# A weight sum of the gate-and-up units: formed by an accumulating transfer instead of by a VectorE addition

## What is computed

```python
D_MODEL = 1024
D_FF = 2816
def swiglu(h, w_gu, w_d):
    gu = h @ w_gu                                   # 1024 x 5632
    return (jax.nn.silu(gu[..., :D_FF]) * gu[..., D_FF:]) @ w_d

    # once in each layer
    hp = hp + swiglu(rms_norm(hp, norm_ffn[layer]), w_gate_up[layer], w_down[layer])
    hs = hs + swiglu(rms_norm(hs, norm_ffn[layer]), w_gate_up[layer], w_down[layer])
```

## Time and profile before

| | us |
|---|---|
| median of 3 timed runs | 1315.87 |
| lowest and highest of them | 1315.61, 1326.59 |
| the profiled execution, its time | 1321.13 |
| the profiled execution, its span from the first to the last instruction | 1319.6 |

### The profile page before, as it was taken

The page is one execution under the profiler, slowest core; times in us unless marked ns, Lnnn a source line. Parts: engine busy times, 40 slices in busy tenths (PEclk is TensorE's granted clock), DMA queues, the critical chain, the costliest instruction groups (busy, mean ns, idle before and its releaser), DMA issues.

```text
span 1319.6 us, 26871 instructions
## 1 busy us (share of the span) xinstructions
PE 1223.9 (93%) x10559; PEld 1008.9 (76%) x10559; DVE 1054.8 (80%) x1741; ACT 685.8 (52%) x1179; POOL 357.2 (27%) x571
## 2 busy tenths in 40 slices
PE   8999996999999889999999999999689999998997
PEld 7767585787787767778888888887568787787886
DVE  6446667899999967777877878777579999998885
ACT  6243556455555544336554655545555555654543
POOL 1004312100001124446455554553211000011230
PEclk9999997999999999999999999999989999998998
DMA  8658545777777699421133231232357777766992
GB/s 265 213 186 278 154 144 104 200 186 166 197 175 160 131 208 225 95 87 58 34 97 97 65 97 45 85 97 81 112 145 192 204 178 168 194 148 124 203 184 78
DMA packets 126230, 193.37 MB, mean 147 GB/s; under 512 B 7801, under 2 KB 88953, under 8 KB 121882
## 3 DMA queue, kind: packets, MB, share of 16 engines
q1 hardware_dynamic: 96730, 157.06, 37.8%
q0 software_dynamic: 29376, 34.61, 18.2%
HBM read 180.53 MB, written 11.11 MB: 145 GB/s over the span
## 4 chain that ended last, share of the span: by engine, by line
PE 52%; DVE 23%; ACT 11%; issue 6%; DMA 6%; POOL 1%; DVEq 0%; SPq 0%; ACTq 0%; POOLq 0%
PE P L2487 20%; PE P L2536 10%; PE P L2114 7%; DVE wl L1706 7%; ACT wh L1027 4%; DMA arena<-w_gu 3%; DMA arena<-w_dn 3%; DVE arena L1751 2%; PE P L2725 2%; ACT arena L1061 2%; DVE wl L1442 1%; DVE arena L1770 1%; DVE wl L1892 1%; PE P L2711 1%; PE P L2545 1%
## 5 line engine op out<-in xcount | busy, mean ns | idle before, releaser
L2487 PE MATMUL P<-arena,wh 128*128 128x260 f16 x2288 | 399.5, 280 | 51.3 <-DVE arena L1725 23.7
L2487 PE MATMUL P<-arena,wl 128*128 128x260 f16 x1144 | 319.2, 279 | 0.0
L2487 PEld LDWEIGHTS P<-arena,wh 128*128 128x128 f16 x2288 | 223.5, 99 | 100.8 <-issue 32.7
L1027 ACT ACTIVATE wh<-arena 128x1024 f16<-128x1024 f32 (+2 forms) x138 | 123.2, 897 | 136.3 <-PE P L2487 103.4
L2487 PE MATMUL P<-zh,wh 128*128 128x260 f16 x704 | 193.6, 275 | 0.0
L2487 PE MATMUL P<-zh,wl 128*128 128x260 f16 x704 | 192.5, 273 | 0.0
L2487 PE MATMUL P<-zl,wh 128*128 128x260 f16 x704 | 192.4, 273 | 0.0
L1706 DVE SCALAR_TENSOR_TENSOR wl<-arena,wh 128x1024 f16<-128x1024 f32 (+2 forms) x138 | 144.7, 1048 | 33.2 <-ACT wh L1027 32.7
L1706 DVE SCALAR_TENSOR_TENSOR wl<-stage,wh 128x1024 f16<-128x1024 f32 (+2 forms) x116 | 132.0, 1139 | 8.1 <-ACT wh L1027 7.6
L1027 ACT ACTIVATE wh<-stage 128x1024 f16<-128x1024 f32 (+2 forms) x116 | 114.0, 984 | 32.4 <-PE P L2487 25.1
L2487 PEld LDWEIGHTS P<-arena,wl 128*128 128x128 f16 x1144 | 113.0, 99 | 18.9
(11 more groups left out here) (422 smaller groups left out, 2656.3 us busy)
## 6 DMA issues: line engine op xcount, KB each, us to landing
arena<-w_gu SPq DMA_DIRECT2D x56, 512.0 KB, 6.2
stage<-w_in SPq DMA_DIRECT2D x23, 1024.0 KB, 5.3
stage<-w_gu SPq DMA_DIRECT2D x44, 512.0 KB, 5.0
arena<-w_gu POOLq DMA_DIRECT2D x22, 512.0 KB, 5.6
stage<-w_gu POOLq DMA_DIRECT2D x22, 512.0 KB, 7.5
arena<-w_dn SPq DMA_DIRECT2D x28, 384.0 KB, 5.5
arena<-w_dn SPq DMA_DIRECT2D x30, 320.0 KB, 4.9
arena<-cache_k SPq DMA_DIRECT2D x32, 256.0 KB, 3.6
```

The costliest lines, as they stand in the source:

```text
L1027: nc.scalar.activation(ringh[:, o:o + block_words(n)], source(kind, n), ACT.Copy, scale=WS).then_inc(c_hi, 1)
L2487: mm = nc.tensor.matmul(bank, w[:, o:o + 128], x[:, k, :], start=(i in (0, 1, 3) and k == a and w is ringh and x is xh), stop=(k == z - 1 ...
```

## The change

For the gate-and-up units (n < 11) T4 is no longer added by VectorE. GpSimd issues a transfer that adds B21 from memory onto T2 in place, the same kind as for T1 and T3. It waits for the low part of T2(n) (`c_lo`), and, since it counts on the same semaphore as T1's transfers, for all transfers of T1 and T4 that stand before it, T1(n+1) last. It stands at the head of iteration n of GpSimd's loop, ahead of T3(n+1) and T1(n+2); T1(n+2) now waits for T4(n) to have landed. ScalarE's high part of T4 waits for the transfer instead of for VectorE. The down units keep the VectorE addition. The load of B21 by SyncE stays, as B21 is an operand by itself too. The counts on `t_sum` and `t1_sum` are renumbered accordingly.

```diff
+SUMS = [(k, n) for n in range(NU) for k in ("T2", "T4") if k == "T2" or n >= NG]
+SUM_AT = {x: i + 1 for i, x in enumerate(SUMS)}
+ADDS = [("T1", 0), ("T1", 1)] + [(k, m) for n in range(NU) for k, m in (("T4", n), ("T1", n + 2))
+                                 if m < NU and (k == "T1" or n < NG)]
+ADD_AT = {x: i + 1 for i, x in enumerate(ADDS)}
...
-                if kind == "T1":
-                    pool.wait_ge(ld1[n % 2], first_load(n % 2, n, layer))
-                    if layer + n > 0:
-                        pool.wait_ge(t1_sum, 16 * (NU * layer + n))
+                if kind in ("T1", "T4"):
+                    if kind == "T1":
+                        pool.wait_ge(ld1[n % 2], first_load(n % 2, n, layer))
+                    else:
+                        pool.wait_ge(c_lo, NB7 * layer + 7 * n + 3)
+                    earlier = len(ADDS) * layer + ADD_AT[kind, n] - 1
+                    if earlier > 0:
+                        pool.wait_ge(t1_sum, 16 * earlier)
                     arrived = t1_sum
...
-                nc.gpsimd.dma_start(rows_of(kind, n), block_of({"T1": "B11", "T3": "B22"}[kind], n, layer),
+                nc.gpsimd.dma_start(rows_of(kind, n), block_of({"T1": "B11", "T3": "B22", "T4": "B21"}[kind], n, layer),
                                     accum_op=ADD).then_inc(arrived, 16)
...
                 for n in range(NU):
+                    if n < NG:
+                        second_term("T4", n, layer)
                     second_term("T3", n + 1, layer)
                     second_term("T1", n + 2, layer)
...
+                elif kind == "T4" and n < NG:
+                    act.wait_ge(t1_sum, 16 * (len(ADDS) * layer + ADD_AT["T4", n]))
                 else:
-                    act.wait_ge(t_sum, 2 * NU * layer + 2 * n + (1 if kind == "T2" else 2))
+                    act.wait_ge(t_sum, len(SUMS) * layer + SUM_AT[kind, n])
...
                 low_part(m, layer)
-                if i == 2:
+                if i == 2 and n >= NG:
                     weight_sum("T4", n, layer)
```

More of the change, by code:

```diff
@@ L1016, in convert @@
                 elif kind == "T1":
-                    act.wait_ge(t1_sum, 16 * (NU * layer + n + 1))
+                    act.wait_ge(t1_sum, 16 * (len(ADDS) * layer + ADD_AT["T1", n]))
                 elif kind == "T3":
@@ L1679, in weight_sum @@
                 if kind == "T2":
-                    dve.wait_ge(t1_sum, 16 * (NU * layer + n + 1))
+                    dve.wait_ge(t1_sum, 16 * (len(ADDS) * layer + ADD_AT["T1", n]))
                     dve.wait_ge(ld2[n % 2], first_load(n % 2, n, layer))
```

## The result

The kernel after takes 1330.88 us (median of 13 runs, 1325.78 to 1336.05), the kernel before, run as often beside it, 1320.97 us (1315.61 to 1329.24). The ratio is 1.008, 95% interval 1.006 to 1.0099: the change costs some 10 us. A later series of runs gave 1.0075 (1.0044 to 1.0106).

A forecast was written before the change was run, and what follows sets the result against it. VectorE was taken to bound the gate-and-up units, TensorE 1.2 us behind. Twenty steady periods at -0.6 us in all and +4 us for the units 0 gave +3.4 us on 1315.87: 1319 us, range 1300 to 1341.

The forecast's parts named there:

- VectorE sets the period, and the addition costs 1.32 us of it: Gate-and-up units: VectorE bounds the 20.33 us period; without the T4 addition VectorE alone would allow 19.01 us.
- the floor of 19.12 us: Gate-and-up units: TensorE, 1.21 us behind VectorE, lets the period fall from 20.33 to 19.12 us and no further.
- T4's transfer waits for T1(n+1), and VectorE for the transfer: Steady units: T1(n+1) must land before T4's transfer goes; VectorE then stands still 1.3 us, giving its saving back.
- R: Time to landing of T4's transfer in a gate-and-up unit: between 5.5 and 7.7 us, taken as 5.5.
- S: Start of TensorE's product i = 6 in a unit; T4's transfer must land by S + 6.99 or VectorE stands still.
- T1's delay of 1.0 us: Steady units: T4's transfer pushes T3's into T1's loads, delaying T1 by 1.0 us, between 0 and 2.5.
- The relation: Steady units, P being the period: 2P = 34.13 + R plus T1's delay, giving 20.3 us, ends 19.8 and 22.2.
- T3's delay costs nothing: Steady units: T3's transfer runs some 2 us later behind T4's, landing near S + 12.7, due only some 13.6 us after.
- The unit 0: First unit of each layer: late T4(0) costs +3.3 us in layer 1, +1.4 in layer 0; +4 taken.
- Ten periods of one kind: Ten periods in each layer, all counted as steady: 20 x (20.3 - 20.33) = -0.6 us.
- crowding: Rival: transfers crowd each other, landing takes 7.0 us and T1 is delayed 1.5; period 21.3, 1341 us; chance 0.25.
- The full gain: Rival: T4's transfer lands before S + 6.99, period 19.12 us, result 1294 us; chance 0.15, full or most of it.

The follow-up runs named there:

- e1: kernel after with neither transfer nor addition of T4 in the gate-and-up units (output lacks that part): 1294.84 us, ratio 0.9825 to the kernel before.
- e4: as e3, with VectorE's product of gate and up moved ahead of T4's low part: 1310.83 us, ratio 0.9915 to the kernel before.
- e7: e4 with the VectorE addition of T4 kept in unit 0 of each layer: 1305.14 us, ratio 0.9893 to the kernel before.
- e10: e4 with the VectorE addition of T4 kept in units 0 and 1 of each layer: 1298.34 us, ratio 0.9824 to the kernel before.
- e3: kernel after with a semaphore of its own for T4's transfer, so it doesn't wait for T1(n+1): 1316.78 us, ratio 0.9967 to the kernel before.
- e11: the kernel before, unchanged, run once more for a second profile: 1314.76 us.
- e8: the kernel after, unchanged, run once more for a second profile: 1331.05 us, ratio 1.0075 to the kernel before.
- e9: kernel after with the VectorE addition of T4 kept in units 0 and 1 of each layer: 1320.64 us, ratio 0.9996 to the kernel before.
- e2: as e1, but B21's bytes are fetched and added onto unused memory, and nothing waits: 1304.14 us, ratio 0.9878 to the kernel before.

## Why the prediction was right, and where it was not

The forecast was +3.4 us, no change within 1%, range 1300 to 1341. Measured: +10 us, 1330.88 us. Sign and class are right, the size is short by 7 us. The kernel before itself came out at 1320.97 in 13 runs, where the forecast started from 1315.87 in 3, so the difference is the fairer measure than the 12 us between 1319 and 1330.88.

- *VectorE sets the period, and the addition costs 1.32 us of it.* Right: 19.01 us was worked out, and 19.0 is the period of e1. The step to it from the 2.47 us of two low parts doesn't hold, as those two start 1.25 us apart; the 1.14 us that was used is the distance from the addition to the next instruction. And the floor of 19.12 us that TensorE was said to set is none: e1 has 18.99, and e4, e7 and e10 have units of 18.87.
- *T4's transfer waits for T1(n+1), and VectorE for the transfer.* Right. The chain of after runs through a load and two transfers, and taking the wait away (e3) shortens the steady periods from about 20.35 to 20.1 and 19.6 us.
- *R.* 5.5 us was taken; 5.94 is measured at 324.03, and the issue is 2.3 us after S. A landing at S + 8.2 against S + 6.99 due gives 1.2 us; VectorE waits 1.33 and 1.72, forecast 1.3.
- *T1's delay of 1.0 us.* Its loads go at 309.16 and it lands at 315.56 + 7.94 = 323.50: 14.3 us against 14.0 before. So the delay is 0.3. The relation also has 0.05 us between T1's landing and T4's issue, where the trace has 0.53 in 16 of 20. With all three in it, 2P = 34.13 + 0.5 + 5.9 + 0.3, P is 20.4; measured 20.35 on average, forecast 20.3. That the forecast came within 0.05 us is partly luck: the three errors of the sizes nearly cancel, and single periods differ by up to 1.9 us.
- *T3's delay costs nothing.* T3 goes right behind T4, 7.4 to 7.8 us to landing instead of 5.5, and ScalarE is shown waiting for it nowhere in the steady units of either profile.
- *The unit 0.* +4 us was forecast for the two heads, from +3.3 and +1.4. Against the very profile that it was worked out from, the heads are +3.6 and +0.3, and the step for layer 1 was good: 6 us of waiting forecast, 6.38 seen. But that profile had a long head in each layer; against the means of both profiles of before they are +6.2, and against the usual 15.4 us layer 1 alone has 6.1 and 6.4. In the first profile ScalarE waited 3.28 us for T3(1) in layer 1, in e11 0.33. The term was short because one profile's head was taken for the head.
- *Ten periods of one kind.* This is the step that failed. The sum took the period from unit 0 to unit 1 as a steady one, worth -0.03 us; it is 21.2 to 22.6 instead of 19.2 to 19.6, +5.4 us for the two. The prediction followed the late T4(0) into VectorE's low parts, and no further than the head. It also holds up ScalarE's copies, and with them TensorE, which stood still for 5.28 us and then ran its next product in 4.97 us at a clock of 0.51 instead of some 2.6. In layer 1 of e8 the chain of waits runs through TensorE alone from the end of this stop to the end of the first period. In after it goes from the slow product to the low part of T2(1) and so to T4(1), which was late once more (VectorE idle for 3.24 us). What the clock's share is, some 2 us in a layer by the rows, is an estimate: no run leaves the stop and not the fall. The timed runs of e9 show that undoing units 0 and 1 takes the loss back, its profile that this came from the heads, and e7 beside e10 that unit 1 has its own share in layer 1.

Of the rivals, crowding is not what holds up the steady units of the change: T1 and T3 can land late for nothing (e2, 151.9 us with the bytes and without), and T4 itself lands in 5.5 to 6.0 us there but for one unit. It is at work at the head, where 5.3 us came with the bytes in e2. And it comes up in the steady units once T4 no longer waits for T1: in e3, e4 and e10 T4's 7 us and more to landing are what is left. The full gain was wrong for the change, and not as a limit: once the wait for T1 is gone, VectorE has other work and the head is left alone, e10 gets a ratio of 0.9824, and the forecast's 1294 us were 0.983 of 1315.87.

The Trainium skill, DMA: Bandwidth & Descriptors, section Anatomy of one DMA — SWDGE (gpsimd) path, would have 3.2 us by its formula for the 512 KB of such a transfer, which is an estimate. The trace doesn't agree: in the steady units of before and after the shortest time to landing of such a transfer is 5.4 us.

## What to carry to other kernels

Moving work from a full engine to a transfer gives little as long as the consumer stands at the same place of the full engine's queue (+10 us here, and with the wait for T1 gone 0.3% less than before). Put the queue's independent work into the time of landing, and look at what shares a semaphore with the new transfer: a count shared by two streams is a wait of one for the other. Once that wait is gone, the two streams can run at the same time and each take longer; look at the time to landing again. Price the first two units of a pipeline by themselves, through the queue of every engine that the late operand holds up, and from more than one profile: here undoing 4 of 22 places took the whole loss back in the timed runs. And count what a stop of TensorE leaves behind it in its clock. The old way was best kept at the head, and the new one used behind it.

## What was not expected of the hardware

Raising the DMA share of a period from 0.74 to 0.89 left all its 16 steady periods at the same 151.9 us for eight (e1, e2), though T3's transfer, behind the new one, took 7.5 us to landing instead of 5.7 (medians). And the stretches in which loads or transfers are on the chain take several lengths in one and the same kernel: the heads 20.2 or 18.3 and 18.0 or 15.4 us, the tails 125 to 135 us. Part of that is TensorE's clock: in layer 1's head the matmuls behind the norm statistics ran at half pace up to 984.6 in the first profile of before, 4.9 us from the first of them, and for 2.8 us in e11. With such variation, only the stretches cut at the same instructions, not the span of a single profile, could be compared here.
